# First slots of a two-block float32 network: order of products, split of the first inputs, place of the squares

## The reference

```python
def rms_norm(x, g):
    y = x * lax.rsqrt(jnp.mean(x * x, axis=-1, keepdims=True) + NORM_EPS) * g
def swiglu(h, w_gate, w_up, w_down):
    return (jax.nn.silu(h @ w_gate) * (h @ w_up)) @ w_down
hdn = swiglu(rms_norm(x, norm_pre[l, 0]), ffn1_w_gate[l], ffn1_w_up[l], ffn1_w_down[l])
x = x + 0.5 * rms_norm(hdn, norm_post[l, 0])
```

## Time and profile before

| | us |
|---|---|
| median of three executions | 1665.07 |
| the three executions | 1664.26, 1665.07, 7304.23 |
| the profiled execution, whole time | 1664.19 |
| its span, first to last instruction | 1662.4 |
| TensorE busy in the span | 1651.9 |
| ACT busy | 920.2 |
| DVE busy | 1218.8 |

### The profile page before, as it was taken

How to read it: one execution, slowest core, us unless ns; L and a number is a source line. 1 busy time by engine, 2 the same in 40 slices (tenths; PEclk the granted TensorE clock), 3 DMA queues, 4 the chain that set the end, 5 groups by cost and what they waited for, 6 DMA issues and landing times.

```text
span 1662.4 us, 22774 instructions
## 1 busy us (share of the span) xinstructions
PE 1651.9 (99%) x8740; PEld 1419.0 (85%) x8740; DVE 1218.8 (73%) x1632; ACT 920.2 (55%) x1396; POOL 148.9 (9%) x210
## 2 busy tenths in 40 slices
PE   9999999999999999999999999999999999999998
PEld 7888888888888888888899888888888889988887
DVE  6888776788889777776788776655766668986564
ACT  6655577645555455545566455545544458655453
POOL 1100100000211001020010010100002011310000
PEclk9999999999999999999999999999999999999999
DMA  8987553787859876787555457554667546357561
GB/s 296 333 264 261 168 192 103 243 292 260 284 178 326 268 247 221 249 304 257 194 170 189 160 177 262 195 191 144 222 215 247 191 142 203 110 177 241 189 194 66
DMA packets 99356, 358.47 MB, mean 216 GB/s; under 512 B 11184, under 2 KB 11696, under 8 KB 99248
## 3 DMA queue, kind: packets, MB, share of 16 engines
q1 hardware_dynamic: 92736, 334.73, 59.8%
q0 software_dynamic: 6368, 22.21, 4.2%
q10 hardware_dynamic: 144, 0.07, 0.0%
HBM read 355.85 MB, written 1.12 MB: 215 GB/s over the span
## 4 chain that ended last, share of the span: by engine, by line
PE 94%; DVE 3%; DMA 1%; ACT 1%; issue 1%; SPq 0%; DVEq 0%; POOLq 0%; POOL 0%; ACTq 0%
PE dn L549 29%; PE gu L503 21%; PE tp L533 11%; PE gu L533 11%; PE gu L538 6%; PE tp L538 6%; PE dn L518 3%; PE tp L466 1%; PE dn L533 1%; DVE w_lo L1790 1%; DMA raw<-in_weights 1%; PE dn L503 1%; PE dn L538 0%; PE tp L645 0%; DMA x<-in_x_in 0%
## 5 line engine op out<-in xcount | busy, mean ns | idle before, releaser
L1790 DVE TENSOR_TENSOR w_lo<-raw,w_hi 128x1024 fp32r<-128x1024 f32 x518 | 635.0, 1237 | 301.6 <-ACT w_hi L1151 297.1
L1151 ACT ACTIVATE w_hi<-raw 128x1024 fp32r<-128x1024 f32 x520 | 547.5, 1056 | 461.6 <-PE dn L549 140.4
L503 PE MATMUL gu<-w_hi,hT 128*128 128x512 f32 x1056 | 328.8, 392 | 1.7 <-DVE w_lo L1783 1.2
L549 PE MATMUL dn<-w_hi,actT_hi 128*128 128x512 f32 x608 | 239.2, 393 | 0.0
L549 PE MATMUL dn<-w_hi,actT_lo 128*128 128x512 f32 x608 | 237.4, 390 | 0.0
L549 PE MATMUL dn<-w_lo,actT_hi 128*128 128x512 f32 x608 | 236.9, 390 | 0.0
L503 PEld LDWEIGHTS gu<-w_hi,hT 128*128 128x128 f32 x1056 | 195.5, 188 | 42.8 <-DVE hT L1798 1.7
L503 PE MATMUL gu<-w_lo,hT 128*128 128x512 f32 x528 | 205.8, 390 | 0.0
L533 PE MATMUL gu<-hT,w_hi 128*128 128x512 f32 x832 | 199.1, 391 | 0.3 <-DVE hT L1798 0.3
L533 PE MATMUL tp<-hT,w_hi 128*128 128x512 f32 x832 | 199.0, 391 | 0.0
L533 PEld LDWEIGHTS gu<-hT,w_hi 128*128 128x128 f32 x832 | 155.1, 188 | 33.0 <-DVE hT L1798 1.0
(11 more groups left out here) (354 smaller groups left out, 1844.0 us busy)
## 6 DMA issues: line engine op xcount, KB each, us to landing
raw<-in_weights SPq DMA_DIRECT2D x561, 512.0 KB, 4.4
arena<-in_ada_w SPq DMA_DIRECT2D x72, 512.0 KB, 4.4
post_row<-in_post_rows POOLq DMA_DIRECT2D x10, 512.0 KB, 5.6
pre_row<-in_pre_rows POOLq DMA_DIRECT2D x10, 512.0 KB, 7.0
mod_row<-mod POOLq DMA_DIRECT2D x9, 512.0 KB, 9.9
shift_row<-mod POOLq DMA_DIRECT2D x5, 512.0 KB, 8.7
x<-in_x_in SPq DMA_DIRECT2D x4, 256.0 KB, 6.2
arena<-in_c_rows POOLq DMA_DIRECT2D x2, 512.0 KB, 9.1
```

The source lines that it names most:

```text
L503: m = pe.matmul(bank, h[:, k, t * P:(t + 1) * P], w[:, r, kk * 512:(kk + 1) * 512], start=k == 0 and q == 0, stop=k == KT - 1 and q == 2)
L549: m = pe.matmul(dn[:, t, c], a[:, k, :], w[:, r, c], start=start and q == 0, stop=stop and q == 2)
L1151: act.activation(o, i, ACT.Copy, **kw).then_inc(done, 1)
L1790: dve.tensor_tensor(w_lo[:, r, :], raw[:, n % RAW, :], w_hi[:, r, :].bitcast(F32), ALU.subtract).then_inc(lo_ready, 1)
```

## The change

- TensorE does three warming matmuls where it did four, and then the products of slots 0 and 1 in the order in which their operands are made: each product waits for its own half of `w_hi` or `w_lo` and for the high or low part of the input, and both tiles are done with one half of slot 1 before the next.
- The high part of hT(0,0) is made by DVE (`tensor_scalar`), not ACT.
- The four squares move behind other work on ACT: (0,0) behind slot 0, (1,0) behind slot 3, (0,1) behind slot 4, (1,1) behind slot 5.
- Slot 1 is fetched in two halves with two semaphores.
- The transposes of tile 1 go to banks of `dn`, which nothing uses until slot 8.

```diff
-WARM, WARM_ON = 5, 4
+WARM, WARM_ON = 5, 3
...
         def in_bank(s, t, half):
+            if t and s == 0:
+                return dn_bank(half)
...
+            def first_load(n):
+                for half, done in enumerate((landed_half[n], landed[n])):
+                    sp.dma_start(raw[:, n, half_of(half)], weights[bass.ts(n, P), half_of(half)]).then_inc(done, 16)
+
             first_rows(0, 0)
-            for half, done in enumerate((landed_half, landed[0])):
-                sp.dma_start(raw[:, 0, half_of(half)], weights[0:P, half_of(half)]).then_inc(done, 16)
+            first_load(0)
             first_rows(1, 0)
-            load(1)
+            first_load(1)
...
+            def first_product(n, kk, t, h, w):
+                k = 2 * n + kk
+                return pe.matmul(gu[:, t, :], h[:, k, t * P:(t + 1) * P], w[:, n, kk * 512:(kk + 1) * 512],
+                                 start=k == 0 and h is hT_hi and w is w_hi, stop=False)
...
                 first_turned(0, 0)
                 keep_warm(WARM_ON)
+                pe.wait_ge(hT_hi_ready, FIRST_HT[0, 0])
+                pe.wait_ge(hi_half, 1)
+                first_product(0, 0, 0, hT_hi, w_hi)
+                pe.wait_ge(lo_half, 1)
+                first_product(0, 0, 0, hT_hi, w_lo)
+                pe.wait_ge(hi_ready, 1)
+                first_product(0, 1, 0, hT_hi, w_hi)
+                first_turned(1, 0)
                 first_there(0, 0)
-                wide_slot(0, 0, {0: gu[:, 0, :]}, used=False, between=lambda: first_turned(1, 0))
-                first_turned(0, 1)
+                for kk in range(2):
+                    first_product(0, kk, 0, hT_lo, w_hi)
+                pe.wait_ge(lo_ready, 1)
+                first_product(0, 1, 0, hT_hi, w_lo)
+                pe.wait_ge(hT_hi_ready, FIRST_HT[1, 0])
+                for kk in range(2):
+                    for w in (w_hi, w_lo):
+                        first_product(0, kk, 1, hT_hi, w)
                 first_there(1, 0)
-                wide_slot(0, 0, {1: gu[:, 1, :]})
-                wide_slot(1, 1, {0: gu[:, 0, :]}, used=False)
+                for kk in range(2):
+                    m = first_product(0, kk, 1, hT_lo, w_hi)
+                m.then_inc(slot_used, 1)
+                for kk, (upper_there, lower_there) in enumerate(((hi_half, lo_half), (hi_ready, lo_ready))):
+                    pe.wait_ge(upper_there, 2)
+                    for t in range(TT):
+                        for h in (hT_hi, hT_lo):
+                            first_product(1, kk, t, h, w_hi)
+                    if kk == 0:
+                        first_turned(0, 1)
+                    pe.wait_ge(lower_there, 2)
+                    for t in range(TT):
+                        m = first_product(1, kk, t, hT_hi, w_lo)
+                m.then_inc(slot_used, 1)
+                first_turned(1, 1)
                 first_there(0, 1)
-                first_turned(1, 1)
-                wide_slot(1, 1, {1: gu[:, 1, :]})
                 wide_slot(2, 2, {0: gu[:, 0, :]}, used=False)
...
+            act.wait_ge(consts, 16)
+            first_upper(0, 0)
+            first_upper(0, 1)
             first_squares(0, 0)
-            in_half_upper(0, 0, 0)
-            act.wait_ge(consts, 16)
-            first_upper()
-            first_squares(1, 0)
             in_half_upper(0, 1, 0)
-            upper(1)
+            first_upper(1, 0)
+            first_upper(1, 1)
             in_half_upper(0, 0, 1)
-            first_squares(0, 1)
             upper(2)
-            first_squares(1, 1)
             in_half_upper(0, 1, 1)
             upper(3)
+            first_squares(1, 0)
             upper(4)
+            first_squares(0, 1)
             upper(5)
+            first_squares(1, 1)
...
+            dve.wait_ge(hT_psum, FIRST_HT[0, 0])
+            dve.tensor_scalar(hT_hi[:, 0:4, 0:P], in_bank(0, 0, 0).rearrange("p (k c) -> p k c", k=4), 1.0, None,
+                              ALU.mult).then_inc(hT_hi_ready, 1)
+            half_rest(0, 0)
+            dve.wait_ge(hT_hi_ready, FIRST_HT[0, 0])
+            in_half_lower(0, 0, 0)
+            half_rest(0, 1)
+            dve.wait_ge(hT_hi_ready, FIRST_HT[1, 0])
+            in_half_lower(0, 1, 0)
+            half_rest(1, 0)
+            half_rest(1, 1)
+            for n, t in ((2, 0), (3, 1)):
+                dve.wait_ge(hT_hi_ready, FIRST_HT[t, 1])
+                in_half_lower(0, t, 1)
                 rest(n)
```

More of the change, by code:

```diff
@@ L279, in build @@
         x_half = [sem(f"x_half_{t}") for t in range(TT)]
-        landed_half, hi_half, lo_half = sem("landed_half"), sem("hi_half"), sem("lo_half")
+        landed_half = [sem(f"landed_half_{n}") for n in range(2)]
+        hi_half, lo_half = sem("hi_half"), sem("lo_half")
         ssq_ready, rstd_ready, x_new, xn_ready = sem("ssq_ready"), sem("rstd_ready"), sem("x_new"), sem("xn_ready")
@@ L487, in half_there, with wide_slot @@
                 pe.wait_ge(hT_lo_ready, 2 * (TT * s + t) + 1)
[L489 to L494, removed]
+            def wide_slot(n, si, banks, used=True):
+                pe.wait_ge(lo_ready, n + 1)
                 r = n % RING
                 for kk in range(2):
-                    if n < 2 and kk:
-                        between()
-                        pe.wait_ge(lo_ready, n + 1)
                     k = 2 * si + kk
@@ L1151, in copy, with first_upper @@
                 act.activation(o, i, ACT.Copy, **kw).then_inc(done, 1)
[L1153 to L1157, removed]
+            def first_upper(n, kk):
+                k, c = FIRST_K[n] + kk, half_of(kk)
+                act.wait_ge((landed_half, landed)[kk][n], 16)
+                copy(w_hi[:, n, c], raw[:, n, c], (hi_half, hi_ready)[kk], scale=pre_cols[:, k:k + 1])
             def upper(n):
@@ L1772, in then, with half_rest @@
                 dve.wait_ge(dve_step, steps[0])
+            def half_rest(n, kk):
+                k, c, r = FIRST_K[n] + kk, half_of(kk), n % RING
+                dve.wait_ge((hi_half, hi_ready)[kk], n + 1 if kk else FIRST_KS[n])
+                dve.scalar_tensor_tensor(w_lo[:, r, c], raw[:, n % RAW, c], pre_cols[:, k:k + 1],
+                                         w_hi[:, r, c].bitcast(F32), ALU.mult, ALU.subtract).then_inc((lo_half, lo_ready)[kk], 1)
             def rest(n):
@@ L1779, in rest @@
                 if n in FIRST_K:
[L1780 to L1784, removed]
+                    for kk in range(2):
+                        half_rest(n, kk)
                     return
@@ L2465, in _ @@
             dve.memset(mod_cols[:, 5 * ADA_Q:, 1:2], 0.0)
-            for n, (t, half) in enumerate(FIRST_HT):
-                dve.wait_ge(hT_hi_ready, FIRST_HT[t, half])
-                in_half_lower(0, t, half)
+            dve.wait_ge(hT_psum, FIRST_HT[0, 0])
[12 more added lines that the diff above has]
+                in_half_lower(0, t, 1)
                 rest(n)
```

## The result

The changed kernel takes 1670.07 us (median of 7 executions, 1669.00 to 1670.65) against 1664.26 for the kernel before: a ratio of 1.0034, 95% interval 1.0025 to 1.0043. It is 5.8 us slower, which is inside the stated range of 1667.5 to 1671.0 and 1.1 us above the 1669.0 given as the likeliest. (One of the executions of before took 7304 us and is left out of the ratio.) The profiled execution took 1670.57 us, with a span of 1668.8.

A forecast was written before the change was run, and what follows sets the result against it. TensorE, busy for 1651.9 of 1662.4 us, was taken to bound the kernel. Order 0.0, loads 0.0 to 0.1 and roots +4.2 us on a base of 1664.7 gave 1669.0 us, range 1667.5 to 1671.0.

The forecast's parts named there:

- The squares are where the time goes: On ACT, late squares delay POOL's roots and the first gate, so slot 4 tile 1 starts 4.23 us later.
- The roots: On POOL, both roots ahead of the first gate take 1.21 us each, since DVE has run out of remainders.
- The first rival: POOL's roots stay as slow as 2.29 us, once more likely than twice: +5.3 us, 1670.0; chance 0.10.
- The base: Starting time of 1664.7 us for the whole kernel, taken between the profiled execution and the median of the runs.
- the likeliest case: Whole kernel at 1668.2 to 1669.5 us, the forecast itself; chance 0.68.
- the second rival: TensorE's clock falls after the long idle ahead of slot 4: +1.5 us more, 1670.4; chance 0.18.
- The order of products gains nothing: On TensorE, slots 0 and 1 end 0.75 us sooner, all given back waiting for slot 2's remainders: 0.0.
- Halves, banks, one warming matmul fewer, the first high part on VectorE: Edits at the start with a cost near nothing; the loads 0.0 to 0.1 us, the others nothing.
- The rival of a gain: ACT's roots ready before 19.2 and slot 2's low part by 14.14 keep the 0.75 us: 1664.0; chance 0.04.

The follow-up runs named there:

- e2: The kernel before with only the four squares moved to their late places on ACT; 1668.84 us, ratio 1.0030.
- e4: The changed kernel with the second to fourth squares moved to where ACT sits idle, ahead of the copy of hT(0,1) at the latest; 1664.34 us, ratio 1.0001.
- e6: The changed kernel with the three late squares together behind slot 3, ahead of slots 4 and 5; 1667.99 us, ratio 1.0022.
- e3: The changed kernel with 15 useless matmuls on zeros in TensorE's wait ahead of slot 4; 1668.33 us, ratio 1.0025.
- e8: e4 with slot 1 fetched whole, as before, in place of in halves; 1664.50 us, ratio 1.0001.
- e9: e7 with the fourth square behind slot 2's copies on ACT; 1663.79 us, ratio 0.9996.
- e5: The changed kernel with ACT's first gate waiting for the first column of roots alone, the second gate for the second; 1668.45 us, ratio 1.0025.
- e10: The kernel before, unchanged, run again as a kernel of its own beside its own runs; 1664.43 us, ratio 1.0000.
- e7: e4 with the transposes of x(0,1) ahead of slot 1's products and the fourth square behind the copy of hT(0,1); 1664.08 us, ratio 1.0000.

## Why the prediction held, point by point

- **The squares are where the time goes.** Shown by e2 (4.65 us with the squares alone) and e4 (the whole loss gone with the squares moved alone). The term was +4.23 us at slot 4 tile 1. Measured from the common zero it is +4.26. Of its parts: last square 20.0 forecast, 19.37 measured; POOL 20.9, 20.25; gate 23.4, 22.83; slot 4 tile 1 26.05, 25.46. All are 0.6 us early, which is x(1,0) landing 0.6 us earlier in this execution. That the sum comes so close is in part luck, for two small errors in it cancel. The transposes of x(1,1) are 0.22 us later from the zero than laid out (6.05 against 5.83). A square and the step to the next copy take 0.61 us (15.69 to 16.30) and not 0.72: the 0.72 came from a copy that in the kernel before probably waited for its transposes, which began at 13.06 only.
- **The roots.** 1.21 us each was taken because DVE would be idle; the trace gives 20.25 to 22.74 for both, 1.24 each with the step between. The first rival (slow roots) didn't occur, and e6 shows what it needs: DVE busy with remainders.
- **The base and the total.** The 1669.0 was 4.2 us on a base of 1664.7. The median of the kernel before is 1664.26, so the base was 0.44 us too high and hid part of what was missing: 1.55 us of clock less 0.44 is the 1.1 us by which the forecast is short. The measured time is outside the 1668.2 to 1669.5 of the likeliest case. By the number alone it would fit the slow roots (1670.0) better than the clock (1670.4), and only the traces tell them apart. The prediction also took 2% as about what a measurement can tell from no change; the intervals here are 0.1% to either side, and a change of 0.34% is clear of them.
- **The clock.** The likeliest case had it stay up, with 0.18 on the second rival and a price of 1.5 us. It fell, and cost 1.55 us (e3). Here the prediction chose the wrong side, and its range held the result only because it was drawn wide enough for this rival. The mechanism and its price were there, but nothing in the trace of before had an idle stretch of more than 1.25 us in the middle of work, and a chance below one half was no more than a guess. The mean clock over the run, 0.999 in both profiles, hardly shows 3.4 us in 1669. The Trainium skill (TensorE: Matmul & The Clock Gate, Part 1) says that an idle array returns to 1.2 GHz; the traces with idle stretches of 2.4, 2.8, 3.1 and 3.7 us agree, each with a fall.
- **The order of products gains nothing.** It was taken as 0.0: 0.75 us ahead at the end of slot 1, all given back ahead of slot 2. By the timeline slots 0 and 1 are done at about 13.69 (13.33 and 0.36 of transposes) against 14.89, of which 0.6 are x(1,0): 0.6 us ahead. The wait for slot 2's remainders follows, and in the comparison from the zero slot 2 is even 0.21 us later. What the prediction didn't say is that the late transposes of x(1,1) push ACT's whole list. With the squares late this is 0.9 to 1.2 us (e2). Most of it is in the 4.23 that was laid out, but it was put down to the squares and needs the new order as well.
- **Halves, banks, one warming matmul fewer, the first high part on VectorE.** Taken as nothing. e8 shows it for the halves. The others weren't tried by themselves; together with the order they come to 0.15 us in e4 (interval from -1.3 to +1.7 us), so that a cost or a gain of some tenths in any of them is not excluded.
- **The rival of a gain** (roots before 19.2 and slot 2 ready by 14.14) needs both conditions, and e9 meets them (its roots are there at 16.4, slot 2 starts at 13.73): even then 0.5 of 0.66 us is gone at slot 5. Slot 2 tile 1 comes 0.29 us late, behind the low part of hT(1,1), which VectorE begins at 14.65, and slot 4 another 0.16.

## What to carry to other kernels

A cheap step that an engine does off the critical path has a due time: the squares cost TensorE nothing until they were put behind work with a later one, and then they cost what the whole chain behind them took, two roots, a gate, a product. Before such a step is moved, lay out the engine's list to the wait that consumes it; here eight durations from one timeline gave the delay within 0.1 us, with errors of 0.1 to 0.2 us in single steps that cancelled. An idle stretch of a few us on TensorE should be priced with the clock's fall behind it, and a reordering near the start should be judged from a landmark that doesn't move with a load's landing.

## What the runs showed of the hardware

- The granted clock fell to 0.50 in all four traces that had an idle stretch of TensorE of 2.4 us or more, in two of them by the first product behind it (e5, e2), in e6 about 1.1 us after slot 4 had begun and in the changed kernel only at about 25.4, 1.5 us after. Idle stretches of up to 1.25 us had no fall behind them.
- The same small load, x(1,0), issued at 2.1 us with the same three loads ahead of it in the queue, landed 4.8 us later in one trace (e6) and 6.1 us later in another (e5).
- At the start five matmuls of 512 columns take 2.50 us, where fifteen of them take 3.56 us in e3's wait, although the clock column reads 1.00 in both stretches. How long this slower pace lasts differs: the next four take 1.18 us in the kernel before and 1.88 us in the same kernel run again (e10), and in e9 the products at 6.04 and 6.46 are still 0.42 apart, where later ones are 0.23 apart. So the column doesn't show the slow start, and the prediction's price of the low clock rests on the pace alone.
- A one-column pow on POOL took 0.56 to 0.57 us with VectorE idle, or at the subtraction that reads one input from PSUM (before at 14.50, e7 at 15.02), and 0.96 to 1.10 us beside VectorE's remainders, whose raw and high parts both lie in SBUF (1.10 in e9).
